# One core, fp32 hybrid encoder: what is dealt out around the last output stage of the mixer, and where the small matmuls of the second norm sit

## Chip, cores and metric

The kernel runs on one core of one Trainium2 chip. The metric is the device time of one execution in microseconds (us), as the median of the runs. PE is TensorE, PEld its weight loads, DVE VectorE, ACT ScalarE, POOL GpSimd, SP the queue that issues the DMAs of the weights.

## What is computed

Two sequences of 1024 tokens of width 1024 go through one encoder layer each, all in fp32. Cut to what matters here:

```python
h = (_rmsnorm(x, g_mix) * (1.0 + scale1) + shift1)
...  # projections, retention, pooling, gates: "merged"
mix_out = jnp.einsum('bsd,de->bse', merged, w_out)
x = x + gate1 * mix_out
h2 = (_rmsnorm(x, g_ffn) * (1.0 + scale2) + shift2)
up = jnp.einsum('bsd,df->bsf', h2, w_up)
up = _dwconv_centred(up, conv_w, conv_b)
act, lin = jnp.split(up, 2, axis=-1)
ffn = jnp.einsum('bsf,fd->bsd', jax.nn.gelu(act) * lin, w_down)
return x + gate2 * ffn
```

The norm of h2 needs, for each token, the sum of squares over all 1024 channels, and so all of x + gate1 * mix_out of that token.

## The kernel before

Activations lie transposed: `xT[seq][:, d, :]` holds 128 channels (block d of 8) by 1024 tokens. A product in fp32 precision is made of three passes on two parts of each operand: a high part (`w_hi`, `m_hi`, `hc_hi`, slot 0 of `f_w`), which ACT makes with an ACTIVATE Copy, and a low part (the remainder, raw minus high), which POOL makes for weights with a subtract of two SBUF operands (`remainder`, L1512; `piece_low`, L1536) and DVE for activations. One matmul streams 128x512.

The mixer runs over four pairs of heads per sequence (`PAIRS`), each with 13 weight blocks (`BLOCKS["mix"]`); blocks 11 and 12 are the halves of w_out. Each engine works an order that is written out by hand in its own function, with semaphores between them, and none overtakes itself. SP issues the loads in order: a block of the mixer is loaded into one of two `w_raw` halves once the block before the last has its low part (`load`). The raw buffers 0 and 1 of the next stage (`f_raw`) are the same memory as `w_raw`.

The last pair's output stage is `tail_out` (PE, its matmuls are on L703). It takes the tokens in halves of 512. Half 0: for each d, three matmuls for the first of the pair's two heads, then, in a second pass, three for the other; at d = 4 of the first pass it turns to block 12 (`weights(where, 12)`). Half 1: for each of W0 to W7, six matmuls into a bank of PSUM that an earlier step has to have read: W0 to W5 wait for updates of half 0, W6 for the fifth update of half 1 (`res_done` at d - 1), W7 for the sixth. DVE updates xT (`tail_update`, L1663, source in PSUM), ACT squares each updated block (`square_mid`, L1195), POOL adds three pairs of squares (L1592) and DVE adds four times more (`square_sum`, L1676, two SBUF operands; each waits for the one before). Then `statistics_of` (PE, L743: four fp32 columns against ones, 8 records of 128x1), `mean_square` (DVE, L1682), the root on POOL (L1516), `diagonal` (DVE, L1635, two SBUF operands), and `spread_mid` (PE, L749, one fp32 product of 128x512, 2 records), which leaves the factor of each token in PSUM. `scale_mid` (DVE, L1691) multiplies by it, `modulate_mid` (ACT, L1204 and L1207) applies scale and shift and copies the high part, `b_low` (DVE, L1699) makes the low part. All of this is done for half 0 and again for half 1.

DVE's order is: eight updates of half 0; four `square_sum`; updates 0 and 1 of half 1; `mean_square(0)`; `diagonal(0)`; updates 2 and 3; `scale_mid` 0 and 1; update 4; `b_low` 0; `scale_mid` 2; update 5; and so on to update 7; then `square_sum` of half 1 with `scale_mid` 4 among them; `scale_mid` 5 to 7 with low parts; `mean_square(1)`; `diagonal(1)`; `scale_mid` 8 to 15. The diff does not touch it.

`opening_sets` (PE, L762) is the first piece of the MLP: weight sets 0 and 1, products with half 0 in two parts of four k-steps, each k-step six matmuls (four high, two low), then the products with half 1, which wait for `scale_mid` 8 and 16 (`mid_scaled`). Its eight weight pieces are the first of `PIECES`, each with a slot of its own (`OPEN_SLOT`): slot 8 is free once the scores of head 1 are made (SC1), 5 after O1, 0 and 1 after GB1 (the last projection), 6 and 7 after BB1 (L1036), 2 and 3 after W7. In `PIECES` a piece is ("open", set, m); m 0 and 1 lie in the first raw block of a set, 2 and 3 in the second. `raw_free` lets a raw block be loaded anew once the low part of its last piece is there.

`statistics_of(mid, 0)` stands behind W2, `spread_mid(mid, 0)` behind W3, `statistics_of(mid, 1)` in the opening behind k = 0 of part 0 for set 1, `spread_mid(mid, 1)` behind k = 0 of part 1 for set 0.

Of the kernel before, what the change touches and what calls it, by code (L numbers as in the profile page):

```python
# [27 lines left out]
KC = D // P  # L28
# [5 lines left out]
PAIRS = HEADS // 2  # L34
# [54 lines left out]
for g in range(1, GROUPS):  # L89
    FFN_ITEMS += [("set", 2 * g), ("down", g - 1), ("set", 2 * g + 1)] if g < GROUPS - 1 else [  # L90
        ("set", 2 * g), ("set", 2 * g + 1), ("down", g - 1), ("down", g)]
PIECES = [("open", n, m) for n, m in ((1, 0), (1, 2), (1, 1), (1, 3), (0, 0), (0, 2), (0, 1), (0, 3))]
OPEN_PIECES = len(PIECES)
OPEN_SLOT = (8, 5, 6, 7, 0, 1, 2, 3)


LOADS = [("set", 0, 0), ("set", 0, 1), ("set", 1, 0), ("set", 1, 1)]
# [56 lines left out]
N_MIX = len(BLOCKS["mix"])  # L154
# [32 lines left out]
def encoder_program(nc, x, c, w_ada, b_ada, g_mix, w_in, decay_f, decay_b, gn_gain, w_pool, pool_scale,  # L187
                    w_out, g_ffn, w_up, conv_w, conv_b, w_down, g_final, consts, y):
    ctx = ExitStack()
    with ctx:  # L190
# [45 lines left out]
        for s in range(N_SEQ):  # L236
            m, a, b = ((96, 112, 128), (16, 0, 96))[s]
# [245 lines left out]
        def filled(where, step):  # L483

            slot, turn = place(where[0], step)
            return full[slot].at(where, turn)
# [17 lines left out]
        def _(sp):  # L504
# [78 lines left out]
            for seq in range(N_SEQ):  # L583
                if seq:
                    sp.wait_ge(*piece_lo.at(("swap", 0, 0), 0))
                for pr in range(PAIRS):
                    where = ("mix", seq, pr)
                    for i in range(N_MIX):
                        mix_block(where, i)
                        if seq == 0 and pr < ADA_PARTS - 1:  # L590
                            for k in {3: (0, 1, 2), 6: (3, 4, 5), 7: (6, 7)}.get(i, ()):
                                late_tile(pr + 1, k)
                        if i == 4 and pr == PAIRS - 1:
                            for l in range(2):
                                up_block(("ffn", seq, 0), 1, l)
                        if i == 6:

                            sp.wait_ge(*mb_done.at(where, 0))
                            sp.dma_start(wpool[:, :].unsqueeze(1), w_pool_v[:, pr:pr + 1, :]).then_inc(wpool_in.sem, 16)
                where = ("ffn", seq, 0)  # L600
                sp.wait_ge(*lo_done.at(where, 0))
                for l in range(2):
                    up_block(where, 0, l)
                for kind, n in FFN_ITEMS:
                    for i in range(2):
                        if kind == "set":
                            up_block(where, n, i)
                        else:
                            down_block(where, n, i)
        @block.tensor  # L610
        def _(pe):
# [81 lines left out]
            def tail_out(where, mid, slot_read):  # L693

                w_slot = [weights(where, 11), None]
                pe.wait_ge(*mhi_done.at(where, 1))
                pe.wait_ge(*mlo_done.at(where, 1))

                def tail_pass(bank, d, half, j, n, start, stop):

                    a, b = ((w_hi, m_hi), (w_lo, m_hi), (w_hi, m_lo))[n]
                    col = j * HALF + (d % 4) * P
                    return pe.matmul(ps_row[:, half_of(bank)], a[:, w_slot[d // 4], col:col + P],  # L703
                                     b[:, j, half_of(half)], start=start, stop=stop)

                for d in range(KC):
                    if d == 4:
                        w_slot[1] = weights(where, 12)
                    if d % 2 == 0:
                        pe.wait_ge(*slot_read[d // 2])  # L710
                    for n in range(3):
                        tail_pass(TAIL_BANKS[d], d, 0, 0, n, n == 0, False)
                pe.wait_ge(*mhi_done.at(where, 2))
                for d in range(KC + 3):
                    if d < KC:
                        for n in range(2):
                            tail_pass(TAIL_BANKS[d], d, 0, 1, n, False, False)
                    if d == 3:
                        pe.wait_ge(*mlo_done.at(where, 2))
                    if d >= 3:  # L720
                        tail_pass(TAIL_BANKS[d - 3], d - 3, 0, 1, 2, False, True).then_inc(tail_done.sem, 1)
                for d in range(KC):
                    bank = TAIL_BANKS_2[d]
                    if d < 6:
                        pe.wait_ge(*tail_res.at(mid, TAIL_BANKS.index(bank) + 1))
                    else:
                        pe.wait_ge(*res_done.at(where, d - 1))
                    for j in range(2):
                        for n in range(3):
                            ins = tail_pass(bank, d, 1, j, n, j == 0 and n == 0, j == 1 and n == 2)  # L730
                    ins.then_inc(full[slot_of(where, f"W{d}")].sem, 1)
                    if d == 2:
                        statistics_of(mid, 0)
                    if d == 3:
                        spread_mid(mid, 0)

            def statistics_of(mid, half):
# [14 lines left out]
            def opening_sets(where, mid):  # L752
# [14 lines left out]
                for part in range(2):  # L767
                    for s in range(2):
                        w = [weight_piece(where, ("open", s, part + 2 * l)) for l in range(2)]
                        for k in range(KQ):  # L770
                            at_k = (part, hc_lo[seq][:, part, :, :], k)
                            pe.wait_ge(*b_hi.at(mid, part * KQ + k + 1))
                            for l in range(2):
                                row(s, l, 0, w[l], *at_k, (0, 1), part == 0 and k == 0, False)
                            pe.wait_ge(*b_lo.at(mid, part * KQ + k + 1))
                            for l in range(2):
                                row(s, l, 0, w[l], *at_k, (2,), False, part == 1 and k == KQ - 1)
                            if part == 0 and s == 1 and k == 0:
                                statistics_of(mid, 1)
                            if part == 1 and s == 0 and k == 0:  # L780
                                spread_mid(mid, 1)
# [321 lines left out]
        def _(act):  # L1103
# [188 lines left out]
            for seq in range(N_SEQ):  # L1292
# [37 lines left out]
                for pr in range(PAIRS):  # L1330
# [41 lines left out]
                    if pr == PAIRS - 1:  # L1372
                        act.wait_ge(*filled(where, "SC1"))
                        piece_high(("ffn", seq, 0), 0)
                        act.wait_ge(*filled(where, "O1"))
                        piece_high(("ffn", seq, 0), 1)
                    act.wait_ge(*ga_done.at(where, 2))
                    tanh_half(where, "GB1", bufB, tb_done)
                    act.wait_ge(*filled(where, "GA1"))
                    split(where, 12)  # L1380
                    if pr == PAIRS - 1:
                        act.wait_ge(*filled(where, "BB1"))
                        piece_high(("ffn", seq, 0), 2)
                        piece_high(("ffn", seq, 0), 3)
                    act.wait_ge(*mg_done.at(where, 2))
                    act.activation(m_hi[:, 1, :], bufA[:, :], ACT.Copy).then_inc(mhi_done.sem, 1)

# [4 lines left out]
                        split(("mix", seq, pr + 1), 1)  # L1392
                mid = ("mid", seq, 0)
                where = ("ffn", seq, 0)
                for q in range(4, 6):
                    piece_high(where, q)
                for d in range(KC):
                    square_mid(mid, seq, 0, d)
                for d in range(2):
                    square_mid(mid, seq, 1, d)  # L1400
                for k in range(2):
# [105 lines left out]
        def _(pool):  # L1507
# [52 lines left out]
            for seq in range(N_SEQ):  # L1560
# [9 lines left out]
                for pr in range(PAIRS):  # L1570
                    where = ("mix", seq, pr)
                    for i in range(2, N_MIX):
                        remainder(where, i)
                        if i in (9, 10):
                            h = i - 9
                            pool.wait_ge(*veps_done.at(where, h + 1))
                            inverse_root(grs[:, :], veps[:, :]).then_inc(grs_done.sem, 1)
                        if i >= 11 and pr == PAIRS - 1:
                            for q in range(2 * (i - 11), 2 * (i - 11) + 2):
                                piece_low(("ffn", seq, 0), q)  # L1580
                    if pr < PAIRS - 1:
                        remainder(("mix", seq, pr + 1), 0)
                        remainder(("mix", seq, pr + 1), 1)
                mid = ("mid", seq, 0)
                where = ("ffn", seq, 0)
                for q in range(4, 6):
                    piece_low(where, q)
                for half in range(2):
                    for a, b in ((0, 1), (2, 3), (4, 5)):
                        pool.wait_ge(*sq_done.at(mid, KC * half + b + 1))  # L1590
                        dst, other = (sq[seq][i][:, half_of(half)] for i in (a, b))
                        pool.tensor_tensor(dst, dst, other, ALU.add).then_inc(sum_low.sem, 1)  # L1592
                    if half == 1:
                        piece_low(where, 6)
                        piece_low(where, 7)
                    pool.wait_ge(*msq_done.at(mid, half + 1))
                    inverse_root(rstd[:, 4 * half:4 * half + 4], msq[:, 4 * half:4 * half + 4]).then_inc(rstd_done.sem, 1)
                for q in range(8, len(PIECES)):
# [679 lines left out]
```

## Time and profile before

| what | us |
|---|---|
| median of 3 runs | 2802.9 (2798.87 to 2802.92) |
| the profiled execution | 2799.77 |
| its span, first to last instruction | 2798.0 |
| PE busy | 2727.0 (97% of the span) |
| DVE, POOL, ACT busy | 1774.9, 1112.6, 825.9 |
| granted TensorE clock, mean | 0.992 |

The span is 1.8 us shorter than the time of its execution. A row of the timeline gives the start, the length, the engine, the line, the operation, its tiles, and in square brackets the idle time of the engine ahead of it with what ended it. Rows that follow each other alike are merged (x8). The region of the change runs from about 672 to 795 us for the first sequence and from about 2040 to 2164 us for the second.

### The profile page before, as it was taken

The page shows a single profiled execution, that of the slowest core. Times are in us where ns is not written, and L with a number is a line of the kernel's source. Part 1 is how long each engine was busy: PE and PEld are TensorE (multiplying, and loading weights), DVE is VectorE, ACT ScalarE, POOL GpSimd, SP SyncE. Part 2 cuts the span into 40 slices and gives each one's busy share as a digit, 9 for nine tenths or more (in the row PEclk, how much of TensorE's full clock was granted, in tenths as well). Part 3 has the DMA queues.
Part 4 walks back from the last instruction along what each step waited for, and adds up shares of the span by engine and source line. Part 5 has one row for each costly group of instructions (what it writes and reads, how often), then busy time and mean ns, then how long its engine had stood idle before and what let it go on. Part 6 is the DMA issues. An engine that isn't in the chain of part 4 may idle for free. (4 is left out here: it accounts for less than half of the span.)

```text
span 2798.0 us, 31867 instructions
## 1 busy us (share of the span) xinstructions
PE 2727.0 (97%) x12703; PEld 2219.9 (79%) x12703; DVE 1774.9 (63%) x2202; ACT 825.9 (30%) x1083; POOL 1112.6 (40%) x704
## 2 busy tenths in 40 slices
PE   6999999999999999999989999999999999999998
PEld 4787788888778888888768888888877788888876
DVE  4653736545877777667776545373768766677766
ACT  5111111111543333333361111111136333333332
POOL 1212121222365666666421221222233656666662
PEclk8999999999999999999999999999999999999999
DMA  6403211120111111111231110112101111112211
GB/s 254 142 31 121 85 46 48 38 66 21 45 45 53 56 58 46 46 61 46 76 130 45 46 48 28 58 31 70 39 23 53 53 46 46 60 46 60 61 38 76
DMA packets 204756, 170.56 MB, mean 61 GB/s; under 512 B 8369, under 2 KB 181697, under 8 KB 201537
## 3 DMA queue, kind: packets, MB, share of 16 engines
q1 hardware_dynamic: 199713, 150.69, 17.2%
q10 hardware_dynamic: 4896, 17.83, 1.7%
q8 instruction: 102, 1.67, 0.3%
q14 instruction: 45, 0.37, 0.0%
HBM read 160.10 MB, written 8.39 MB: 60 GB/s over the span
## 5 line engine op out<-in xcount | busy, mean ns | idle before, releaser
L1536 POOL TENSOR_TENSOR f_w<-f_raw,f_w 128x512 fp32r<-128x512 f32 x376 | 544.8, 1462 | 523.9 <-ACT f_w L1187 523.2
L658 PE MATMUL ps<-hc_hi,f_w 128*128 128x512 f32 x2240 | 692.0, 390 | 1.6 <-DVE u_sb L1734 1.5
L1512 POOL TENSOR_TENSOR w_split<-w_raw,w_split 128x1024 fp32r<-128x1024 f32 x104 | 255.6, 2461 | 859.9 <-ACT w_split L1107 859.9
L622 PE MATMUL ps<-h_hi,w_split 128*128 128x512 f32 x1792 | 500.8, 394 | 0.0
L658 PEld LDWEIGHTS ps<-hc_hi,f_w 128*128 128x128 f32 x2240 | 418.5, 188 | 94.0 <-DVE u_sb L1734 6.4
L820 PE MATMUL ps<-a_split,f_w 128*128 128x512 f32 x1920 | 449.2, 392 | 12.8 <-DVE xT L1788 10.2
L820 PEld LDWEIGHTS ps<-a_split,f_w 128*128 128x128 f32 x1920 | 357.1, 188 | 102.0 <-DVE xT L1788 24.5
L658 PE MATMUL ps<-hc_lo,f_w 128*128 128x512 f32 x1120 | 435.9, 389 | 0.0
L622 PEld LDWEIGHTS ps<-h_hi,w_split 128*128 128x128 f32 x1792 | 332.0, 188 | 83.8 <-issue 17.2
L1187 ACT ACTIVATE f_w<-f_raw 128x512 fp32r<-128x512 f32 x376 | 226.1, 623 | 456.1 <-PE ps L820 215.1
L981 PE MATMUL ps<-w_split,h_hi 128*128 128x512 f32 x1024 | 318.2, 392 | 10.6 <-DVE h_lo L1653 10.6
L1788 DVE SCALAR_TENSOR_TENSOR xT<-ps,modT,xT 128x512 f32<-128x512 f32 x352 | 251.7, 743 | 78.7 <-PE ps L820 78.5
L622 PE MATMUL ps<-h_lo,w_split 128*128 128x512 f32 x896 | 276.5, 390 | 0.0
L658 PEld LDWEIGHTS ps<-hc_lo,f_w 128*128 128x128 f32 x1120 | 210.2, 188 | 44.0
L981 PEld LDWEIGHTS ps<-w_split,h_hi 128*128 128x128 f32 x1024 | 194.0, 190 | 51.4 <-DVE y_sb L1626 5.8
L1751 DVE SCALAR_TENSOR_TENSOR cv<-u_sb,convT,cv 128x1023 f32<-128x1023 f32 x80 | 148.5, 1856 | 85.5 <-ACT cv L1242 84.7
L981 PE MATMUL ps<-w_split,h_lo 128*128 128x512 f32 x512 | 200.6, 392 | 0.0
L622 PEld LDWEIGHTS ps<-h_lo,w_split 128*128 128x128 f32 x896 | 168.2, 188 | 35.8
L1107 ACT ACTIVATE w_split<-w_raw 128x1024 fp32r<-128x1024 f32 x104 | 108.8, 1054 | 233.8 <-PE ps L981 134.6
L1953 DVE TENSOR_TENSOR bufA<-ps,cst 128x512 f32<-128x512 f32 x32 | 22.1, 692 | 231.9 <-PE ps L981 229.7
L1758 DVE SCALAR_TENSOR_TENSOR cv<-u_sb,convT,cv 128x1023 f32<-128x1023 f32 x80 | 157.2, 1966 | 2.1
L1117 ACT ACTIVATE bufB<-ps 128x1024 f32<-128x1024 f32 x32 | 32.8, 1024 | 373.7 <-PE ps L622 373.7
(205 smaller groups left out, 3321.1 us busy)
## 6 DMA issues: line engine op xcount, KB each, us to landing
f_raw<-in_w_up SPq DMA_DIRECT2D x168, 256.0 KB, 3.2
w_raw<-in_w_in SPq DMA_DIRECT2D x56, 512.0 KB, 3.8
f_raw<-in_w_down SPq DMA_DIRECT2D x88, 256.0 KB, 3.2
ada_late<-in_w_ada SPq DMA_DIRECT2D x16, 1024.0 KB, 5.6
xin<-in_x ACTq DMA_DIRECT2D x16, 512.0 KB, 5.9
ada<-in_w_ada SPq DMA_DIRECT2D x8, 1024.0 KB, 8.9
w_raw<-in_w_in SPq DMA_DIRECT2D x64, 128.0 KB, 2.6
w_raw<-in_w_in SPq DMA_DIRECT2D x32, 256.0 KB, 3.1
```

The source lines that it names most:

```text
L622: ins = pe.matmul(ps[:, slot, b * HALF:(b + 1) * HALF], w[:, w_slot, col:col + P], a[:, k, b * HALF:(b + 1) * HALF], start=first and n == ...
L658: ins = pe.matmul(ps_row[:, half_of(PRODUCT_BANK[i])], a[:, cols], b, start=k == 0 and n == 0, stop=k == KQ - 1 and n == 2)
L820: ins = pe.matmul(ps[:, slot, cols], a[:, d * P:(d + 1) * P], b[:, cols], start=j == 0 and n == 0, stop=j == 1 and n == 2)
L981: ins = pe.matmul(ps[:, slot, (t % 2) * HALF:(t % 2 + 1) * HALF], a[:, k, t * P:(t + 1) * P], w[:, ws, col:col + HALF], start=k == 0 and n ...
L1107: act.activation(w_hi[:, BLOCKS[where[0]][i][1], :], w_raw[:, i % 2, :], ACT.Copy).then_inc(hi_done.sem, 1)
L1117: act.activation(dst[:, :], ps[:, slot, :], ACT.Tanh, scale=0.5).then_inc(t.sem, 1)
L1187: act.activation(piece_slot(q)[:, 0, :], piece_raw(q), ACT.Copy).then_inc(piece_hi.sem, 1)
L1512: pool.tensor_tensor(w_lo[:, ws, :], w_raw[:, i % 2, :], w_hi[:, ws, :].bitcast(F32), ALU.subtract).then_inc(lo_done.sem, 1)
L1536: pool.tensor_tensor(piece_slot(q)[:, 1, :], piece_raw(q), piece_slot(q)[:, 0, :].bitcast(F32), ALU.subtract).then_inc(piece_lo.sem, 1)
L1751: dve.scalar_tensor_tensor(dst[:, 1:S], u[:, 0:S - 1], col[:, 0:1], dst[:, 1:S], ALU.mult, ALU.add).then_inc(side_tap[l].sem, 1)
L1758: dve.scalar_tensor_tensor(dst[:, 0:S - 1], u[:, 1:S], col[:, 2:3], dst[:, 0:S - 1], ALU.mult, ALU.add).then_inc(side_tap[l].sem, 1)
L1788: dve.scalar_tensor_tensor(xT[seq][:, d, cols], ps[:, 2 + r % 2, cols], modT[:, seq, 40 + d:41 + d], xT[seq][:, d, cols], ALU.mult, ALU.ad ...
```

## The change

In `PIECES` the second set-1 piece of each part and the set-0 pieces change places: (1,0), (1,2), (0,2), (0,0), (1,1), (1,3), (0,1), (0,3), with their slots. SP loads the second raw block of set 0 as soon as block 11 has its low part, and the first when block 12 has. ACT splits block 12 ahead of the last tanh (GB1), makes piece 2 before the high part of the merged activation, piece 3 after it, and pieces 4 and 5 behind the eight squares of half 0 and a wait for BB1. POOL makes low parts 0 and 1 behind block 11's remainder, 2 and 3 behind block 12's, 4 and 5 between the three adds of half 0 and its root, 6 and 7 as before. PE has the small matmuls of half 0 behind W3, their spread behind W5, and the small matmuls of half 1 behind k = 1.

```diff
-PIECES = [("open", n, m) for n, m in ((1, 0), (1, 2), (1, 1), (1, 3), (0, 0), (0, 2), (0, 1), (0, 3))]
+PIECES = [("open", n, m) for n, m in ((1, 0), (1, 2), (0, 2), (0, 0), (1, 1), (1, 3), (0, 1), (0, 3))]
-OPEN_SLOT = (8, 5, 6, 7, 0, 1, 2, 3)
+OPEN_SLOT = (8, 5, 1, 0, 6, 7, 2, 3)
...
                 where = ("ffn", seq, 0)
+                sp.wait_ge(*lo_done.at(("mix", seq, PAIRS - 1), N_MIX - 1))
+                up_block(where, 0, 1)
                 sp.wait_ge(*lo_done.at(where, 0))
-                for l in range(2):
-                    up_block(where, 0, l)
+                up_block(where, 0, 0)
...
-                    if d == 2:
+                    if d == 3:
                         statistics_of(mid, 0)
-                    if d == 3:
+                    if d == 5:
                         spread_mid(mid, 0)
...
-                            if part == 0 and s == 1 and k == 0:
+                            if part == 0 and s == 1 and k == 1:
                                 statistics_of(mid, 1)
...
+                    act.wait_ge(*filled(where, "GA1"))
+                    split(where, 12)
                     act.wait_ge(*ga_done.at(where, 2))
                     tanh_half(where, "GB1", bufB, tb_done)
-                    act.wait_ge(*filled(where, "GA1"))
-                    split(where, 12)
                     if pr == PAIRS - 1:
-                        act.wait_ge(*filled(where, "BB1"))
                         piece_high(("ffn", seq, 0), 2)
-                        piece_high(("ffn", seq, 0), 3)
                     act.wait_ge(*mg_done.at(where, 2))
...
+                piece_high(where, 3)
+                for d in range(KC):
+                    square_mid(mid, seq, 0, d)
+                act.wait_ge(*filled(("mix", seq, PAIRS - 1), "BB1"))
                 for q in range(4, 6):
                     piece_high(where, q)
-                for d in range(KC):
-                    square_mid(mid, seq, 0, d)
...
-                        if i >= 11 and pr == PAIRS - 1:
-                            for q in range(2 * (i - 11), 2 * (i - 11) + 2):
+                        if i == 11 and pr == PAIRS - 1:
+                            for q in range(2):
                                 piece_low(("ffn", seq, 0), q)
...
-                for q in range(4, 6):
+                for q in range(2, 4):
                     piece_low(where, q)
                 for half in range(2):
...
-                    if half == 1:
-                        piece_low(where, 6)
-                        piece_low(where, 7)
+                    for q in ((4, 5), (6, 7))[half]:
+                        piece_low(where, q)
                     pool.wait_ge(*msq_done.at(mid, half + 1))
```

## Rows read from the trace of the kernel before

**Rows 1.** The page, part 1: busy time and share of each engine.

```profile
PE 2727.0 (97%) x12703; PEld 2219.9 (79%) x12703; DVE 1774.9 (63%) x2202; ACT 825.9 (30%) x1083; POOL 1112.6 (40%) x704
```

**Rows 2.** Waits of PE over the whole run: total us, times, longest.

```profile
PE ps L743 <- DVE sq L1676: 7.6, 4, 2.4
...
PE ps L749 <- DVE diag_mid L1635: 1.9, 3, 0.8
```

**Rows 3.** Timeline of PE, first sequence: start, length, operation, idle before.

```profile
698.04 0.70 PE L703 MATMUL ps<-m_hi,w_split 128*128 128x512 f32 x2 [0.17 <-issue]
...
712.99 1.05 PE L743 MATMUL ps<-ones,sq 128*128 128x1 f32 x8 [2.43 <-DVE sq L1676]
...
717.27 1.17 PE L749 MATMUL ps<-diag_mid,ones 128*128 128x512 f32 x2 [0.52 <-DVE diag_mid L1635]
...
722.72 0.73 PE L703 MATMUL ps<-m_hi,w_split 128*128 128x512 f32 x2 [0.16 <-DVE xT L1663]
...
724.22 1.07 PE L762 MATMUL ps<-hc_hi,f_w 128*128 128x512 f32 x4
...
732.91 1.05 PE L743 MATMUL ps<-ones,sq 128*128 128x1 f32 x8 [1.73 <-DVE sq L1676]
...
752.69 5.05 PE L762 MATMUL ps<-hc_hi,f_w 128*128 128x512 f32 x21 [0.43 <-DVE h_full L1691]
```

**Rows 4.** Timeline of DVE, first sequence.

```profile
703.12 5.45 DVE L1663 SCALAR_TENSOR_TENSOR xT<-ps,modT,xT 128x512 f32<-128x512 f32 x8 [0.61 <-PE ps L703]
...
715.46 1.76 DVE L1635 TENSOR_TENSOR diag_mid<-cst,rstd 128x512 f32<-128x512 f32 x1 [1.13 <-POOL rstd L1516]
...
718.48 1.29 DVE L1691 TENSOR_TENSOR h_full<-xT,ps 128x512 f32<-128x512 f32 x2
719.86 0.75 DVE L1663 SCALAR_TENSOR_TENSOR xT<-ps,modT,xT 128x512 f32<-128x512 f32 x1
...
721.92 0.75 DVE L1663 SCALAR_TENSOR_TENSOR xT<-ps,modT,xT 128x512 f32<-128x512 f32 x1
...
728.73 4.13 DVE L1676 TENSOR_TENSOR sq<-sq,sq 128x512 f32<-128x512 f32 x3
...
736.98 0.15 DVE L1682 TENSOR_SCALAR msq<-ps 128x4 f32<-128x4 f32 x1
```

**Rows 5.** Timeline of POOL and DVE in narrow windows: instructions that overlap.

```profile
708.69 1.31 POOL L1592 TENSOR_TENSOR sq<-sq,sq 128x512 f32<-128x512 f32 x1
...
708.79 1.76 DVE L1676 TENSOR_TENSOR sq<-sq,sq 128x512 f32<-128x512 f32 x1 [0.22 <-POOL sq L1592]
...
710.65 0.69 DVE L1676 TENSOR_TENSOR sq<-sq,sq 128x512 f32<-128x512 f32 x1
...
728.53 1.29 POOL L1536 TENSOR_TENSOR f_w<-f_raw,f_w 128x512 fp32r<-128x512 f32 x1 [3.01 <-ACT f_w L1187]
...
729.77 1.74 POOL L1536 TENSOR_TENSOR f_w<-f_raw,f_w 128x512 fp32r<-128x512 f32 x1
```

**Rows 6.** Timeline of ACT, first sequence: the last piece ahead of the squares.

```profile
704.22 0.63 ACT L1187 ACTIVATE f_w<-f_raw 128x512 fp32r<-128x512 f32 x1 [2.01 <-DMA f_raw<-in_w_up]
```

**Rows 7.** Timeline of PE, second sequence.

```profile
2081.62 1.05 PE L743 MATMUL ps<-ones,sq 128*128 128x1 f32 x8 [2.32 <-DVE sq L1676]
...
2083.38 0.63 PE L703 MATMUL ps<-m_lo,w_split 128*128 128x512 f32 x1
2083.80 1.05 PE L703 MATMUL ps<-m_hi,w_split 128*128 128x512 f32 x2
...
2085.90 2.08 PE L749 MATMUL ps<-diag_mid,ones 128*128 128x512 f32 x2 [0.62 <-DVE diag_mid L1635]
```

**Rows 8.** Windows: PE, PEld, DVE, ACT, POOL busy (x instructions), granted clock, DMA.

```profile
714.00:717.30 3.30, 2.78 (x8) 1.68 (x7) 2.17 (x4) 0.89 (x2) 2.27 (x2) 0.50 0.00 0
...
734.50:737.80 3.30, 3.30 (x10) 2.55 (x9) 2.20 (x5) 3.24 (x6) 0.59 (x1) 0.50 0.99 333
...
2082.80:2089.50 6.70, 6.08 (x13) 3.56 (x13) 4.52 (x7) 1.48 (x3) 2.26 (x2) 0.50 0.01 2
```

## Prediction

> **What bounds it now.** The page first: PE is busy 97% of the span [rows 1], so only the gaps of PE, and what its clock loses behind them, can be won. The waits of PE next: the small matmuls of the second norm (L743) wait 7.6 us in four places for DVE's sums of squares, the spreads (L749) 1.9 us [rows 2]. The timeline of PE around them then gives, for the first sequence, 0.17 us at 698.04, 2.43 at 712.99, 0.52 at 717.27, 0.16 at 722.72, 1.73 at 732.91 and 0.43 at 752.69, together 5.4 us [rows 3]. Behind three of the four small products the granted clock is 0.50, the 1.2 GHz level, for 3.3, 3.3 and 6.7 us [rows 8]. A matmul starts 0.42 to 0.43 us after the one before it there [rows 7] and 0.23 otherwise ((5.05 - 0.39) / 20, with 0.39 us for the last one's own length) [rows 3]. So the prize in sight is some 11 us of gaps over both sequences and about 6 us of clock.
>
> What the reader should see next is who sets those gaps. The chain is: eight updates of xT on DVE from 703.12, 0.68 apart; squares on ACT just behind them; three adds on POOL; four sums on DVE, the last ending at 712.99, when PE starts [rows 3, 4, 6]. From there: mean square, root on POOL, diagonal to 717.22, spread to 718.44, first scaling at 718.48 [rows 3, 4]. From 718.48 DVE works nearly without a break to the sums of half 1 (the last three end at 732.86), the mean square at 736.98 and the scalings for which PE waits at 752.69. PE's order has slack on this chain in some places and none at 752.69. My thesis is that this stage is set by the DVE chain, and that PE's position in it matters only where DVE waits for PE.
>
> **Block 12 split early, pieces 2 and 3 early.** Today PE waits 0.17 us at 698.04, at the turn to block 12, whose low part POOL has just finished; split ahead of the last tanh, which waits for the last projection (48 matmuls of 0.227, 10.9 us), it is ready long before. That wait goes, in both sequences: -0.17 us each, and the first update comes at 702.95. SP issues the same four DMAs, each earlier, while PE works at that projection; its one new wait, on block 11's low part, has nothing behind it but these loads, and I cost them at nothing. If that cover were missing, piece 3 would be late on ACT ahead of the squares: today piece 5 waits 2.01 us for its DMA until 704.22 [rows 6], with the first update at 703.86, so that is under 1 us.
>
> **Adds and sums of half 0.** Today ACT starts the squares only behind piece 5 of 704.22 to 704.85, POOL the adds behind its low part, and the third add runs 708.69 to 710.00 [rows 5, 6]. Afterwards squares follow the updates: the sixth update ends at 702.95 + 6 x 0.68 + 0.07 = 707.1, its square (0.63, as the piece of rows 6, which is of the same size) at 707.75, and the third add (1.3) at 709.1. Rows 5 show what an add does to DVE: the first sum, 0.69 when alone, starts 0.1 us behind POOL's add and takes 1.76; it ends 0.55 us after POOL does. So it would end at 709.7, today 710.55: 0.9 us gained.
>
> But POOL now has low parts 4 and 5 here. The eighth update ends at 708.4 and its square at 709.1; ACT makes piece 4 right behind it, to 709.7 (0.63 [rows 6]), so POOL begins its low part at 709.7, when DVE wants its second sum. The trace has this meeting once already, in half 1: low part 728.53 to 729.82, a sum wanted at 728.73, the next low part stretched from 1.29 to 1.74 [rows 5], and three sums in 4.13 us [rows 4], where alone they are 2.3 (0.80 apart, the spacing of the last three of half 0 up to 712.99). Two low parts between the sums: second sum ends 711.0 + 0.6 = 711.6, low part 5 is held up to 712.85, third sum ends 713.4, fourth at 714.2. Against 712.99 that is **+1.2 us**; with no meeting at all it would be 709.7 + 3 x 0.80 = 712.1, -0.9 us. I take +1.2, since the rows of half 1 are the same two instructions with the same operands; -0.9 stays as the lower bound. The Trainium skill says the same of the mechanism (SBUF — State Buffer, "Who interferes with whom"): a DVE instruction with two SBUF inputs and a GpSimd one that reads SBUF take turns on a shared port, the later one blocked for the whole instruction. By that rule, which speaks against low parts 4 and 5 in this place, the term is the +1.2; if the two ran side by side it would be the -0.9, and rows 5 agree with the rule.
>
> **Small matmuls behind W3.** PE reaches them 6 x 0.227 = 1.36 us later, at 711.6, and waits to 714.2: 2.6 us, no less than the 2.43 of today. The end of the wait is DVE's, so moving them costs nothing and gains nothing while the sums are late.
>
> **Spread behind W5.** The sums to the end of the diagonal are 4.23 us (712.99 to 717.22 [rows 3, 4]), so it is ready at 718.45. PE has 12 matmuls ahead of the spread from 715.15: 2.7 us at full clock (717.9, in time), 5.1 if all run at half. The spread alone is about 1.0 us at full clock (half of the 2.08 that it takes at the half clock [rows 7]), so it ends near 719.5, today 718.44. Then comes the new wait. W6 needs update 4 of half 1 and W7 update 5, and DVE does these behind scalings 0 and 1, which wait for the spread: update 4 ends 2.1 us and update 5 4.2 us after the first scaling starts (718.48 to 720.61 and 722.67 [rows 4]). Today W4 and W5 lie over that; now PE stands some 2.2 us ahead of W6 (719.5 to 721.7), and W7 starts near 723.8 against 722.72. The opening starts near 725.3 against 724.22. Queued behind PE's wait are W6, W7 and the opening; behind DVE's, everything.
>
> **Half 1.** All of DVE's chain is later by what the spread is. PE reaches the small product at 725.3 + 36 x 0.227 = 733.5 instead of after 6.8 us of opening, and waits about 0.5 instead of 1.73 us. Its result isn't read before 736.98 [rows 4], 3 us after the product, so one unit later is free. The gain of PE here is lost again at the spread and at 752.69, where the scalings set the start. POOL's low parts 6 and 7 and the loads of set 2 behind them keep their places.
>
> **The sum.** First sequence: spread ends 1.1 us later, with the clock low for a while in front of it 0.1 to 1.2 more; I take +1.2. Second: today its spread takes 2.08 us at half clock; afterwards +1.2 for the sums, between -1.0 and +1.0 for the clock; I take +0.8. Together **+2.0 us** on the profiled execution's 2799.8 (span 2798.0 and 1.8 around it): 2801.8. The median of the three runs is 3.1 us above that execution, so on it 2804.9. A difference under 0.2%, 5.6 us here, is about what a measurement of this kernel can't tell from none.
>
> **Rivals.**
> 1. The low parts miss the sums (ACT makes pieces 4 and 5 too late, or the two don't hold each other up). Then -0.9 us per sequence, and about -1 us for a spread at full clock in the second: -2.8, 2800.1. For: the sums would start 0.8 us earlier than today. Against: ACT is idle for pieces 4 and 5 just then, and rows 5. Chance 0.20.
> 2. PE's order sets the stage after all. Then the four waits of L743 shrink by 1.36 us or to nothing (1.36 x 3, and the 1.1 us that is left of 7.6 after 2.43, 2.32 and 1.73 [rows 2, 3, 7]), those of L749 go (1.9), and with them the drops of the clock (13.3 us at half for 6.2 us of work lost): -13, about 2790. For: PE is at 97%. Against: 2.2 us of new wait at W6, and the gap at 752.69 has DVE ahead of it. Chance 0.11.
> 3. Slower: the clock. PE stands 2.6 us, then runs only the small product, and 12 matmuls and the spread follow while today 6 stand between. If the 1.2 GHz level holds over all of them, as it did for 6.7 us in the second sequence [rows 8], the spread starts at 715.15 + 5.1 = 720.3 and ends at 722.4: +3.9 us. In the second sequence, where today's is slow too, +3.0. Together +6.9: 2809.8. It decides once the low stretch lasts over 3.3 us, the time that the diagonal needs. Against: with work in hand PE got its clock back after 3.3 us at 717.3. Chance 0.09.
> That the change does not do what it says I exclude: the orders are explicit.
>
> **How the numbers follow.** Forecast 0.60, rivals 0.20, 0.11, 0.09. Rival 1 and the forecast lie within 0.2%, except for a sliver. So faster 0.12, same 0.79, slower 0.09. The likeliest is 2804.9. The range goes down to rival 1 less the 4 us by which the runs shown differ (2796.1) and up to rival 3 (2809.8).
>
> **What would show it.** Right: DVE's sums of half 0 again 1.6 us and more long between POOL's L1536, ending near 714; PE idle some 2.6 us before L743 and over 2 us in front of W6 (L703 <- DVE xT L1663), where DVE's update costs PE 0.16 today; 0.5 before the second L743; 0.4 or more still at the half-1 products. Wrong: sums ending before 713, the wait at W6 absent, or PE entering the opening before 724.

## The result, and the profile after

The changed kernel takes 2807.03 us in the median of 17 runs (2803.16 to 2809.86), the kernel before 2802.02 us in 17 (2798.87 to 2807.5). The ratio is 1.0016, 95% interval 1.001 to 1.0023: 5.0 us slower, under the 0.2% named in the prediction, but not hidden by the noise, as the prediction took such a difference to be. The profiled execution has a span of 2805.2 us against 2798.0.

The page, busy times; then the waits of PE over the whole run (total, times, longest), which answer to [rows 1] and [rows 2]:

```profile
PE 2731.7 (97%) x12703; PEld 2225.8 (79%) x12703; DVE 1766.6 (63%) x2202; ACT 826.9 (29%) x1083; POOL 1113.0 (40%) x704
```

```profile
PE ps L744 <- DVE sq L1676: 4.5, 2, 2.3
PE ps L704 <- DVE xT L1663: 4.1, 2, 2.0
PE ps L750 <- DVE diag_mid L1635: 4.0, 2, 2.0
```

The wait for the sums is down from 7.6 to 4.5 us, and more than that has turned up elsewhere: 4.1 us in front of W6 (an update of xT), where it was 0.2, and 4.0 us in front of the spreads, where it was 1.9. Nothing of the wait was won: the three together are 12.6 us, where they were 9.7. The timeline of PE after, first sequence and then second, beside [rows 3, 7]:

```profile
714.09 1.87 PE L744 MATMUL ps<-ones,sq 128*128 128x1 f32 x8 [2.27 <-DVE sq L1676]
...
720.92 1.02 PE L750 MATMUL ps<-diag_mid,ones 128*128 128x512 f32 x2
...
723.98 1.11 PE L704 MATMUL ps<-m_hi,w_split 128*128 128x512 f32 x2 [2.04 <-DVE xT L1663]
...
736.61 0.95 PE L744 MATMUL ps<-ones,sq 128*128 128x1 f32 x8
...
743.76 1.27 PE L750 MATMUL ps<-diag_mid,ones 128*128 128x512 f32 x2 [2.01 <-DVE diag_mid L1635]
...
2087.76 1.05 PE L744 MATMUL ps<-ones,sq 128*128 128x1 f32 x8 [2.27 <-DVE sq L1676]
...
2093.09 1.02 PE L750 MATMUL ps<-diag_mid,ones 128*128 128x512 f32 x2
...
2096.15 1.12 PE L704 MATMUL ps<-m_hi,w_split 128*128 128x512 f32 x2 [2.04 <-DVE xT L1663]
```

The gap of 0.17 us at the turn to block 12 is gone. The gap in front of the product of half 0 is 2.27 us (2.43 before), though PE comes to it six matmuls later. In the first sequence the product itself takes 1.87 instead of 1.05 us, and from its start to the start of the spread it is 6.8 us, where it was 4.3. The windows say why (columns as in [rows 8]; the 0.50 or 1.00 is the granted clock):

```profile
714.00:720.70 6.70, 6.61 (x20) 5.55 (x21) 4.61 (x7) 1.26 (x2) 2.27 (x2) 0.50 0.00 1
720.80:724.10 3.30, 1.26 (x5) 0.39 (x4) 1.95 (x3) 1.37 (x3) 0.00 (x0) 1.00 0.00 0
724.20:727.50 3.30, 3.30 (x9) 2.49 (x9) 2.84 (x5) 3.27 (x6) 1.29 (x1) 0.50 0.00 0
744.70:748.00 3.30, 3.30 (x9) 2.50 (x8) 1.99 (x4) 2.15 (x3) 1.42 (x2) 0.50 0.00 0
2089.50:2092.80 3.30, 3.30 (x9) 2.56 (x8) 2.58 (x3) 0.19 (x1) 1.94 (x2) 0.50 0.00 0
```

In the first sequence the 1.2 GHz level holds for 6.7 us behind the first wait and for 3.3 us behind each of the two others (W6 and the spread of half 1). In the second it comes only behind the small product and holds for 3.3 us (the last row). And the timelines of DVE and POOL, in narrow windows, show the sums of half 0 (beside [rows 4, 5]):

```profile
708.38 1.36 DVE L1676 TENSOR_TENSOR sq<-sq,sq 128x512 f32<-128x512 f32 x1
...
709.85 1.72 DVE L1676 TENSOR_TENSOR sq<-sq,sq 128x512 f32<-128x512 f32 x1
...
711.67 1.57 DVE L1676 TENSOR_TENSOR sq<-sq,sq 128x512 f32<-128x512 f32 x1
...
713.35 0.69 DVE L1676 TENSOR_TENSOR sq<-sq,sq 128x512 f32<-128x512 f32 x1
```

```profile
709.73 2.96 POOL L1537 TENSOR_TENSOR f_w_open<-f_raw_open,f_w_open 128x512 fp32r<-128x512 f32 x2 [0.54 <-ACT f_w_open L1188]
```

Low parts 4 and 5 lie from 709.73 to 712.69, and the two sums that fall on them take 1.72 and 1.57 us, where the last takes 0.69. The first sum, 1.36 us, falls on POOL's third add.

To compare executions I count from the start of the last matmul of BB1, the last thing that both orders share, in the profiles' narrow windows. Times in us, first sequence / second sequence:

| | before | after |
|---|---|---|
| first update of half 0 starts | 8.60 / 8.61 | 8.15 / 8.15 |
| fourth sum of half 0 ends | 18.42 / 18.34 | 19.17 / 19.17 |
| diagonal of half 0 ends | 22.70 / 22.62 | 24.19 / 23.46 |
| spread of half 0 ends | 23.92 / 24.75 | 27.08 / 25.58 |
| fourth sum of half 1 ends | 38.34 / 39.17 | 41.48 / 39.99 |
| spread of half 1 ends | 47.50 / 47.73 | 50.17 / 48.69 |
| first matmul of the first down product | 98.42 / 98.67 | 101.80 / 100.31 |

Over the stage that is +3.4 us in the first and +1.6 us in the second sequence: together 5.0 us, as between the medians. That the two meet so closely is chance in part: the table compares one execution of each kernel, and the interval of the ratio allows 2.8 to 6.4 us. (The other 2.2 us by which the profiled spans differ lie outside the stage, most of it between the sequences.)

### The profile page after: what moved, and what is told of

Read it like the earlier page. It is cut to its first block and busy times, and to the rows that moved or that the text cites. A ratio compares the mean times of both kernels' runs of the same rounds, so it can differ in the third digit from the quotient of the medians.

```text
span 2805.2 us, 31867 instructions
## 1 busy us (share of the span) xinstructions
PE 2731.7 (97%) x12703; PEld 2225.8 (79%) x12703; DVE 1766.6 (63%) x2202; ACT 826.9 (29%) x1083; POOL 1113.0 (40%) x704
```

## The experiments

The theory going in: POOL's low parts 4 and 5 hold DVE's sums up, the wait that this leaves on PE costs the clock, and with 12 matmuls in front of the spread the low clock reaches the chain. The rival: the new places of PE's small products are the loss by themselves. Each run is compared with its own runs of the kernel before on the same chip.

**Low parts 4 and 5 behind the root.** The changed kernel with:

```diff
-                    for q in ((4, 5), (6, 7))[half]:
-                        piece_low(where, q)
+                    if half == 1:
+                        piece_low(where, 6)
+                        piece_low(where, 7)
                     pool.wait_ge(*msq_done.at(mid, half + 1))
                     inverse_root(...).then_inc(rstd_done.sem, 1)
+                    if half == 0:
+                        piece_low(where, 4)
+                        piece_low(where, 5)
```

> The changed kernel with one edit: POOL makes low parts 4 and 5 behind the root of half 0, not between its adds and the root. Theory (the two low parts hold DVE's sums up, and the long wait that follows costs the clock): from the first update to the end of the fourth sum 9.0 us instead of 11.0; PE's wait before the small product of half 0 under 0.6 us instead of 2.27; no drop of the clock behind it, so the spread ends some 4.6 us (first sequence) and 3.1 us (second) earlier, counted from BB1; W6 still waits 2 us. Time near 2800. Rival (the place of the spread behind W5 is the loss, whatever POOL does): the sums come earlier but the spread's end doesn't, time stays within 1.5 us of 2807.

Measured: 2799.68 us, ratio to before 0.9992 (0.9983 to 1.0001), some 0.24% or 6.7 us under the changed kernel. Timelines of PE, DVE and POOL of this kernel:

```profile
713.47 1.05 PE L744 MATMUL ps<-ones,sq 128*128 128x1 f32 x8 [0.37 <-DVE sq L1680]
717.76 1.13 PE L750 MATMUL ps<-diag_mid,ones 128*128 128x512 f32 x2 [0.37 <-DVE diag_mid L1639]
720.93 0.73 PE L704 MATMUL ps<-m_hi,w_split 128*128 128x512 f32 x2 [2.05 <-DVE xT L1667]
```

```profile
709.66 3.75 DVE L1680 TENSOR_TENSOR sq<-sq,sq 128x512 f32<-128x512 f32 x4
```

```profile
715.87 2.96 POOL L1537 TENSOR_TENSOR f_w_open<-f_raw_open,f_w_open 128x512 fp32r<-128x512 f32 x2
```

The four sums take 3.75 us instead of 5.66 and end 17.27 us behind BB1 (9.1 from the first update). PE's gap is 0.37 us, the clock stays up through product and spread (in the first sequence it falls at 722, behind the wait at W6; in the second, behind the same wait, it does not fall at all), and the spread ends at 22.74 in both sequences: 4.3 and 2.8 us earlier. The wait at W6 is still 2.05 us. So the place of the two low parts is worth the whole loss and more; PE's new order is not what makes the kernel slower.

**PE's order, taken alone and taken back.** The kernel before with PE's three moves (the two PE hunks of the change and nothing else):

> The kernel before with PE's three moves alone (small product behind W3, spread behind W5, the product of half 1 behind k = 1); ACT, POOL and SP as before. Theory (POOL's low parts are what makes the product late): sums end 9.8 us after the first update as before, PE waits 1.1 us instead of 2.4, and with the clock kept the spread ends where it did before; W6 waits 2 us. Time within 1.5 us of before, 2802. Rival (PE's moves are the loss by themselves): 2805 to 2807.

Measured: 2800.87 us, 0.9994 (0.9986 to 1.0003). The first gap is 0.64 us instead of 2.43 (1.1 was expected: in this execution the sums also ended 0.3 to 0.4 us sooner than in the profile of the kernel before), the clock does not fall in the first sequence, and W6 waits 2.05 us. By themselves the moves cost nothing that can be measured. Then the changed kernel with the same moves undone:

> The changed kernel with PE's three moves undone (small product behind W2, spread behind W3, product of half 1 behind k = 0); ACT, POOL and SP as changed. Theory: the sums still take 11.0 us from the first update, since POOL's low parts 4 and 5 stand among them; PE waits 3.6 us for them instead of 2.27 and the clock falls in both sequences, but only six matmuls stand in front of the spread, which so ends 24.5 to 25.9 us behind BB1. Time 2804 to 2806. Rival (PE's moves are the loss): time back at 2802 or under.

Measured: 2806.28 us, 1.0011 (1.0002 to 1.002). PE's timeline:

```profile
715.93 1.56 PE L744 MATMUL ps<-ones,sq 128*128 128x1 f32 x8 [3.62 <-DVE sq L1676]
720.64 2.07 PE L750 MATMUL ps<-diag_mid,ones 128*128 128x512 f32 x2 [0.38 <-DVE diag_mid L1635]
```

The gap is the 3.6 us expected, and the low clock stretches product and spread. The spread ends at 26.00 and 25.89, 1.1 us before and 0.3 us behind where it ends with the moves in (27.08 and 25.58). And with both edits, low parts behind the root and PE undone:

> The changed kernel with low parts 4 and 5 behind the root of half 0 and PE's three moves undone. Theory: the sums take 9.1 us from the first update as in the run with the low parts moved alone; PE's wait before the small product is 1.7 us instead of 0.37 and its clock may fall once or twice, but the spread waits for the diagonal alone, so that it ends 22.7 to 23.7 us behind BB1, at best equal to that run. Time 2799.5 to 2802. If PE's moves cost something by themselves, this run is faster than the one with the low parts moved alone (2799.7) by over 1 us; if they help by keeping the clock, slower.

Measured: 2800.96 us, 0.9992 (0.9983 to 1.0001). The sums end at 17.26, the spread at 23.94 and 23.66, 1.2 and 0.9 us behind the run with the moves in, its clock having fallen in both sequences. The ratio is the same as that of the run with the moves in, so the time does not tell the two apart. In the profiles the moves bring the spread a little forward: the gap before the product is 1.73 us without them and 0.37 with them.

**Is it the meeting, or the place?** The changed kernel with one wait on POOL ahead of low parts 4 and 5, which stay in front of the root:

```diff
+                    if half == 0:
+                        pool.wait_ge(*sum_all.at(mid, 4))
                     for q in ((4, 5), (6, 7))[half]:
                         piece_low(where, q)
```

> The changed kernel with one wait more: POOL makes low parts 4 and 5 in the same place, between its adds and the root of half 0, but only once the fourth sum is there. Theory (DVE and POOL keep each other out while both read SBUF): the sums take 9.1 us from the first update, PE's wait before the product shrinks to 0.4 us, but the two low parts (2.6 us) now stand in front of the root, 1.4 us more than the product and the mean square take, so the diagonal ends 23.0 us behind BB1: between the changed kernel (23.5 to 24.2) and the run with the low parts behind the root (21.6). Time 2802 to 2803.5. Rival (ACT's pieces 4 and 5 or another thing delays the sums, and not the meeting): the sums stay at 11.0 us.

Measured: 2802.54 us, 0.9997 (0.9988 to 1.0006). DVE and POOL:

```profile
709.30 3.75 DVE L1678 TENSOR_TENSOR sq<-sq,sq 128x512 f32<-128x512 f32 x4
```

```profile
713.13 2.54 POOL L1537 TENSOR_TENSOR f_w_open<-f_raw_open,f_w_open 128x512 fp32r<-128x512 f32 x2 [3.02 <-DVE sq L1678]
715.63 1.02 POOL L1517 TENSOR_TENSOR rstd<-msq,mhalf 128x4 f32<-128x4 f32 x1
```

The same instructions in the same order on each engine, only not at the same time: the sums are back at 3.75 us, the low parts at 2.54. Now the root queues behind them, and the diagonal ends at 22.64, 1.1 us later than with the low parts behind the root. ACT's work is the same in both kernels (it starts pieces 4 and 5 at 14.17 and 14.69 us behind BB1 in either), so it is the overlap of the two engines that stretched the sums.

**What the clock costs.** The changed kernel with ten matmuls ahead of the wait, written to a bank that the product overwrites:

```diff
                     if d == 3:
+                        for n in range(10):
+                            pe.matmul(ps_row[:, half_of(STAT_BANK[0])], w_hi[:, w_slot[0], 0:P],
+                                      m_hi[:, 0, half_of(1)], start=True, stop=True)
                         statistics_of(mid, 0)
```

> The changed kernel with ten matmuls of 128x512 more behind W3, ahead of the wait for DVE's sums; their result is overwritten and read by nobody. They fill the 2.27 us wait and add none. Theory of the clock (of the 5 us, about 3 come from the 1.2 GHz level over the small product and the 12 matmuls of W4 and W5): the granted clock stays 1.0 from 710 to 722 us, the small product takes 1.05 us instead of 1.87 in the first sequence, the spread ends 24.5 us after BB1 instead of 27.1 and 25.6; time near 2803.5. Rival (all of it is DVE's late sums, the clock is hidden): time stays at 2807.

Measured: 2804.1 us, 1.0004 (0.9995 to 1.0013). The same window as above, and PE:

```profile
714.00:720.70 6.70, 4.48 (x19) 2.81 (x18) 5.57 (x9) 2.30 (x4) 2.28 (x2) 1.00 0.00 0
```

```profile
713.44 1.05 PE L747 MATMUL ps<-ones,sq 128*128 128x1 f32 x8
717.74 1.13 PE L753 MATMUL ps<-diag_mid,ones 128*128 128x512 f32 x2 [0.39 <-DVE diag_mid L1638]
```

DVE's sums are as late as in the changed kernel (19.19), but the clock is 1.00, the product takes 1.05 us, and the spread ends at 24.66 in both sequences, 2.4 and 0.9 us earlier. Useless work took some 3 us off (2807.0 to 2804.1, 1.0016 to 1.0004; the intervals just overlap), which agrees with the 3.3 us at the spreads: that is what the low clock costs the changed kernel. Not all of it is difference, for the kernel before pays too: in its second sequence the way from diagonal to the end of the spread is 2.1 us at the low clock, where it is 1.2 in this run. Of the 4.0 us by which the two spreads of half 0 end later than before, late sums are then 1.6 and the clock 2.4.

**The wait at W6.** The changed kernel with DVE's updates 4 and 5 of half 1 ahead of scalings 0 and 1:

> The changed kernel with one edit on DVE: updates 4 and 5 of half 1 ahead of scalings 0 and 1 instead of behind them. Theory (PE's new wait at W6 is a circle: PE holds the spread back behind W5 while DVE holds W6's update back behind the spread): the 2.04 us wait at W6 goes in both sequences, DVE's 1.6 us idle ahead of the first scaling takes up the two updates, and the sums of half 1 end 13.0 us after the spread instead of 14.4; time about 2804. Rival (the wait at W6 is covered, since the opening waits for DVE anyway): W6 waits no more but the opening waits instead, and the sums of half 1 stay 14.4 us behind the spread; time 2807.

Measured: 2806.25 us, 1.0012 (1.0003 to 1.0021), and the expectation was wrong. DVE:

```profile
719.10 2.71 DVE L1663 SCALAR_TENSOR_TENSOR xT<-ps,modT,xT 128x512 f32<-128x512 f32 x4
721.74 1.27 DVE L1691 TENSOR_TENSOR h_full<-xT,ps 128x512 f32<-128x512 f32 x2
723.96 0.69 DVE L1699 TENSOR_TENSOR hc_lo<-h_full,hc_hi 128x512 fp32r<-128x512 f32 x1 [0.95 <-ACT hc_hi L1208]
```

In the first sequence the clock happened to stay up behind the same wait of 2.27 us:

```profile
714.00:722.00 8.00, 5.82 (x25) 4.04 (x26) 6.76 (x11) 1.26 (x2) 2.28 (x2) 1.00 0.00 1
```

So the spread ended at 720.35, and DVE was not idle in front of the scaling: the four updates stood in its way, and the sums of half 1 ended 15.7 us behind the spread instead of 14.4 (14.8 in the second sequence, where the clock fell). The wait at W6 fell to 0.85 us in the first sequence and went in the second; PE then waited for ACT's high parts instead. From the first scaling to the eighth it is 17.1 us, as in the changed kernel, though DVE has two updates less between them. So the wait at W6 was covered, and DVE's 0.95 us of idle time in front of the low part suggests what sets the pace behind the spread: scaling on DVE, modulation on ACT and the low part on DVE again. No run took that round apart.

**The same meeting in half 1.** The kernel with low parts 4 and 5 behind the root, and POOL waiting for the sums of half 1:

```diff
                     if half == 1:
+                        pool.wait_ge(*sum_all.at(mid, 8))
                         piece_low(where, 6)
                         piece_low(where, 7)
```

> The changed kernel with low parts 4 and 5 behind the root of half 0, and with POOL waiting for the fourth sum of half 1 before it makes low parts 6 and 7. Theory (the same hold-up costs half 1 as much as half 0): the last three sums of half 1 take 2.4 us instead of 4.13, so that the diagonal of half 1 and what follows come up to 1.7 us earlier in each sequence, less what the low parts then take from DVE's b_low; time 2797 to 2798.5. Rival (the scalings and low parts of half 1 are paced by ACT, and the sums have room): the sums come early and the diagonal stays where it is, 44.5 us behind BB1; time 2799.7.

Measured: 2797.27 us, 0.9979 (0.997 to 0.9988), and once more beside two others:

> The kernel with low parts 4 and 5 behind the root and 6 and 7 behind the sums of half 1 once more, beside the two that build on it: 0.9979 of before within its interval, near 2797.

2796.07 us, 0.9979 (0.997 to 0.9987). DVE in the first of the two runs:

```profile
729.21 2.27 DVE L1681 TENSOR_TENSOR sq<-sq,sq 128x512 f32<-128x512 f32 x3
...
732.00 1.41 DVE L1704 TENSOR_TENSOR hc_lo<-h_full,hc_hi 128x512 fp32r<-128x512 f32 x1
```

The three sums take 2.27 us instead of 4.13 and end 1.86 us earlier; the low parts of POOL now stretch two low parts of DVE instead (1.41 for 0.69 us), and the diagonal of half 1 comes 1.0 us earlier. In the first sequence little of it is left: the low clock behind W6 lasts 6.8 us, PE comes to the spread of half 1 only a microsecond behind the diagonal, and the spread ends 0.1 us earlier than with low parts 4 and 5 moved alone (1.1 us in the second). This kernel is faster than the kernel before by 0.2% and than the changed one by nearly 0.4%. Against the run with low parts 4 and 5 moved alone the gain is less sure, since the two intervals touch at 0.9983 to 0.9988.

Two refinements followed, the first with `k == 0` again for the product of half 1, the second with that and update 4 between scalings 0 and 1, update 5 behind scaling 1:

> The kernel with low parts 6 and 7 behind the sums of half 1, and with the small product of half 1 back behind k = 0. There the sums end 35.3 us behind BB1 and PE comes to the product only at 36.7 to 39.5, so DVE's mean square now waits 0.4 us for PE. Theory: behind k = 0 the product comes in time, the diagonal of half 1 is up to 0.4 us earlier, time 0.3 to 0.8 us less than the kernel with k = 1 run beside it. Rival: PE's own place (43.5 to 44.6 us at the spread) sets the rest; no difference.

> As the kernel with low parts 6 and 7 behind the sums and k = 0, and DVE makes update 4 of half 1 between scalings 0 and 1, and update 5 between scaling 1 and the first b_low. Nothing is put in front of the first scaling, and ACT needs the second scaling only 2.4 us after the first. Theory: the wait at W6 shrinks from 2.05 to 1.4 us, the one at W7 goes, and the sums of half 1 keep their distance from the spread; PE is 0.6 to 1.2 us earlier at the spread of half 1 where it is last there; time 0 to 1 us less than without it. Rival: the first b_low comes 0.7 us later and the pace of ACT and DVE with it; no gain or a loss up to 1 us.

Measured: 2796.68 us, 0.9982 (0.9973 to 0.9991), and 2795.77 us, 0.9979 (0.9969 to 0.9988). In the second the wait at W6 is 1.45 us as expected and the sums keep their distance, but neither can be told from the kernel they build on, so that of the first the rival held and the 0.3 to 0.8 us expected did not come: the diagonal of half 1 ends at 43.4 to 43.5 us in all three.

One meeting of this kind is in every kernel here, the fastest too, and no run has removed it. POOL starts an add or a low part as soon as it has made the root, 0.04 to 0.06 us ahead of DVE's diagonal, and in every profile each diagonal of the second norm takes 1.75 to 1.80 us (as in [rows 4]). Another instruction of the same line and shape in the kernel before, with only a narrow POOL instruction beside it, takes 0.68:

```profile
1428.15 0.68 DVE L1635 TENSOR_TENSOR diag<-cst,rstd 128x512 f32<-128x512 f32 x1
```

That is some 1.1 us on the chain at each of four diagonals, an estimate from these rows that is not tested.

## Why the prediction was right, and what it mis-sized

The direction, the range and the cause held: slower, by less than 0.2%, because POOL's low parts 4 and 5 meet DVE's sums. The size did not: the forecast was 2 us, the measured difference 5.0. Step by step:

- **Block 12 split early.** Forecast -0.17 us; the first update comes 0.45 us earlier counted from BB1. The gap also cost the slow start of the matmuls behind it, as the starts show (697.48 to 698.04 where 0.23 is usual). Pieces 2 and 3 and the loads were free, as said.
- **Sums of half 0.** Forecast: the fourth sum ends 1.2 us later than before, 11.25 us behind the first update (702.95 to 714.2). Measured: 0.8 us later, 11.0 behind the first update (9.8 before); the sooner first update makes up most of the rest. The order of events is that of the prediction: first sum 1.36, second held up, third held up, fourth alone. The two runs that part POOL from DVE make it shown and not only argued. Rival 1 is excluded by the same rows.
- **Product behind W3.** PE was to wait 2.6 us; it waited 2.27. (From its own terms the prediction should have had 2.45: 710.56 less 0.17 plus 1.36 is 711.75, not 711.6.)
- **Spread behind W5.** This is the term that was mis-sized: "with the clock low for a while in front of it 0.1 to 1.2 more". In the profile the clock fell before the small product had run, stayed low for 6.7 us, and took 0.8 us at the product, which the prediction had not counted at all, and 1.9 us passed between diagonal and spread, above the 1.2 at most of the forecast. The spread ended 3.2 us later than before in the first sequence where +1.2 was forecast; in the second, where the low stretch was 3.3 us, 0.8 later as forecast. That agreement is luck: the forecast had +1.2 for the sums and a gain of 0.4 from the clock, measured were +0.8 for the sums and no gain (2.1 us from diagonal to the end of the spread in both kernels). Rival 3 had the mechanism at +3.9 and +3.0, and happened in one sequence, short of the spread itself. With the clock kept by filler work the kernel is at 2804.1; the forecast was 2804.9.
- **W6.** Forecast 2.2 us of wait, measured 2.04; forecast as a consequence of the order and without cost of its own beyond the chain, which the run of the updates confirms.
- **Half 1.** The distance from the spread of half 0 to the sums of half 1 is 14.4 us in both kernels, and moving the product to k = 1 was free. Two signs named in the prediction did not come. PE was to wait 0.5 us for the sums of half 1 and waits for nothing: the clock falls behind the wait at W6, so that PE comes to the product only when the sums are there (where the clock holds behind W6, in the first sequence of the filler run, the wait is 0.40 us). And at the products with half 1 a wait of 0.4 or more was to stay, but it is gone (0.43 before). PE waits 2.01 us for the spread of half 1, where the prediction did say that its gain is lost again, and what it did not foresee is that the clock falls there a third time, and that PE then comes late to the second half. From the first t_mid of DVE (its first instruction behind the last scaling and low part of half 1) to the first down product it is 38.9 us after in both sequences, 38.15 before: 0.7 us more each. The same distance is 38.3 to 39.0 in the three sequences of other runs (with the filler, and with POOL's wait for the sums of half 0) whose clock fell right at that spread, and 38.1 to 38.2 in every other sequence of the traces. So the link to the clock is seen in five sequences, but an experiment of its own it has not had.

Rival 2 (PE's order sets the stage) is refuted from both sides: the moves alone bring nothing measurable where 13 us were to be won, and undoing them in the changed kernel gives nothing measurable back.

## What to carry to other kernels

Before work is put into an idle stretch of POOL, look at what DVE does there: if it is a chain of instructions with two SBUF operands, much of POOL's time is added to the chain (1.9 us here for two low parts of 1.29), and the gap that looked free is not. Moving a waiting matmul back does not shorten a wait whose end another engine sets, it moves it. And a wait of PE has a second price in its clock, which falls due on whatever follows; count that on the chain and not only on PE.

## What the runs showed of the hardware

- A DVE sum of 128x512 with two SBUF operands takes 0.69 us alone and 1.35 to 1.77 us when a POOL add or subtract of two SBUF operands has begun before it. Each of those in the changed kernel and the one before ends 0.55 us behind the POOL instruction, as the prediction had read it for the first sum. POOL's low part takes 1.29 alone and 1.72 to 1.74 beside DVE. Updates of DVE with a source in PSUM keep their 0.74 us.
- The clock fell to the 1.2 GHz level around a PE wait of 2.27 us and the product behind it, whose eight records have one column each. In the first sequence it had fallen by the end of the wait, and the product took 1.87 us instead of 1.05; in the second only behind the product. With the updates moved, the same wait and product left it up in the first sequence. After a wait of 0.37 us and the same product it stayed up until the next wait, as it did with ten full matmuls in place of the wait. The wait of 2.05 us at W6 was followed by the low level in the first sequence of the run with low parts 4 and 5 behind the root, and not in the second.
- How long the low level lasts varies between sequences of one execution: 6.7 and 3.3 us after the same wait of 2.27 us. What decides it these runs don't show.
